# A three-layer block on one core: C's first values in other banks, dense groups ahead of scores and transposes, and norm roots as log and exp

## What is computed

```python
h = rmsnorm_2(x, pre_mix_w[l])
proj = h @ w_in[l]                       # q_a, k_a, v_a, q_b, k_b, v_b, gates
y_a = diff_attention(q_a, k_a, v_a, lam, subln_w[l], lambda_init)
y_b = neighbourhood_attention_2d(q_b, k_b, v_b, rpb[l])
merged = g_a * (y_a @ w_branch_a[l]) + g_b * (y_b @ w_branch_b[l])
x = x + rmsnorm_2(merged @ w_out[l], post_mix_w[l])
h = rmsnorm_2(x, pre_ffn_w[l])
f = (jax.nn.silu(h @ w_gate[l]) * (h @ w_up[l])) @ w_down[l]
x = x + rmsnorm_2(f, post_ffn_w[l])
```

## Time and profile before

| | us |
|---|---|
| median of 3 runs (lowest to highest) | 2002.32 (2001.63 to 2002.58) |
| profiled execution, its own time | 2001.68 |
| its span | 2000.0 |
| TensorE (PE) busy | 1973.4, 99% of the span |
| VectorE (DVE) busy | 1039.5, 52% |
| ScalarE (ACT) busy | 713.0, 36% |
| GpSimd (POOL) busy | 18.8, 1% |
| mean granted TensorE clock | 0.997 |

### The profile page before, as it was taken

How to read it: one execution, slowest core, us unless ns; L and a number is a source line. 1 busy time by engine, 2 the same in 40 slices (tenths; PEclk the granted TensorE clock), 3 DMA queues, 4 the chain that set the end, 5 groups by cost and what they waited for, 6 DMA issues and landing times.

```text
span 2000.0 us, 25477 instructions
## 1 busy us (share of the span) xinstructions
PE 1973.4 (99%) x9948; PEld 1608.8 (80%) x9948; DVE 1039.5 (52%) x1458; ACT 713.0 (36%) x1058; POOL 18.8 (1%) x57
## 2 busy tenths in 40 slices
PE   9999999999999999999999999999999999999998
PEld 7988888888887777778888887766778998888887
DVE  6354665425465455575434556665445585533544
ACT  5443432212243444442222233444433452223232
POOL 0100000000000000000000000000000000000000
PEclk9999999999999999999999999999999999999999
DMA  4321333343233222233333324112323323233322
GB/s 158 92 72 54 108 84 92 87 116 84 81 108 127 85 80 69 85 85 90 93 111 84 89 83 146 45 64 61 107 70 104 107 64 104 75 106 94 100 71 81
DMA packets 299983, 180.79 MB, mean 90 GB/s; under 512 B 19179, under 2 KB 295764, under 8 KB 299900
## 3 DMA queue, kind: packets, MB, share of 16 engines
q1 hardware_dynamic: 288959, 178.90, 30.7%
q10 hardware_dynamic: 10941, 0.75, 0.4%
HBM read 175.80 MB, written 2.75 MB: 89 GB/s over the span
## 4 chain that ended last, share of the span: by engine, by line
PE 91%; DVE 4%; ACT 3%; issue 1%; DMA 0%; DVEq 0%; ACTq 0%
PE psum L1731 28%; PE psum L1733 27%; PE psum L1732 27%; PE psum L1987 1%; DVE wl L1100 1%; PE psum L1940 1%; PE psum L1949 1%; PE psum L1912 1%; PE psum L1962 1%; PE psum L2024 1%; PE psum L1998 1%; ACT wh L620 1%; PE psum L1879 1%; PE psum L2006 1%; PE psum L2196 0%
## 5 line engine op out<-in xcount | busy, mean ns | idle before, releaser
L1100 DVE TENSOR_TENSOR wl<-stage,wh 128x2048 fp32r<-128x2048 f32 (+2 forms) x170 | 353.0, 2077 | 122.2 <-ACT wh L620 118.8
L620 ACT CAST wh<-stage 128x2048 fp32r<-128x2048 f32 (+2 forms) x164 | 283.4, 1728 | 230.2 <-PE psum L1733 221.0
L1731 PE MATMUL psum<-xl,wh 128*128 128x512 f32 (+1 forms) x768 | 304.9, 397 | 2.1 <-DVE work L1182 1.5
L1731 PE MATMUL psum<-x2l,wh 128*128 128x512 f32 x768 | 302.8, 394 | 1.0 <-DVE wl L1100 0.6
L1733 PE MATMUL psum<-x2h,wh 128*128 128x512 f32 x768 | 299.1, 389 | 0.0
L1732 PE MATMUL psum<-x2h,wl 128*128 128x512 f32 x768 | 299.0, 389 | 0.0
L1733 PE MATMUL psum<-xh,wh 128*128 128x512 f32 (+1 forms) x768 | 293.1, 382 | 0.0
L1732 PE MATMUL psum<-xh,wl 128*128 128x512 f32 (+1 forms) x768 | 292.5, 381 | 0.0
L1731 PE MATMUL psum<-hidl,wh 128*128 128x512 f32 x528 | 205.8, 390 | 2.6 <-DVE wl L1100 2.6
L1732 PE MATMUL psum<-hidh,wl 128*128 128x512 f32 x528 | 205.4, 389 | 0.0
L1733 PE MATMUL psum<-hidh,wh 128*128 128x512 f32 x528 | 205.4, 389 | 0.0
(11 more groups left out here) (344 smaller groups left out, 2621.9 us busy)
## 6 DMA issues: line engine op xcount, KB each, us to landing
stage<-in_ffn_w_gate_dram SPq DMA_DIRECT2D x44, 512.0 KB, 4.1
stage<-in_ffn_w_up_dram SPq DMA_DIRECT2D x44, 512.0 KB, 5.3
stage<-in_w_in_dram SPq DMA_DIRECT2D x40, 512.0 KB, 4.2
stage<-in_ffn_w_down_dram SPq DMA_DIRECT2D x32, 384.0 KB, 3.7
stage<-in_a_w_in_dram SPq DMA_DIRECT2D x22, 512.0 KB, 4.8
stage<-in_w_gate_dram SPq DMA_DIRECT2D x22, 512.0 KB, 4.1
stage<-in_w_up_dram SPq DMA_DIRECT2D x22, 512.0 KB, 5.3
stage<-in_ffn_w_down_dram SPq DMA_DIRECT2D x32, 320.0 KB, 3.6
```

The lines of the kernel that those rows point to most:

```text
L620: nc.scalar.copy(wh[:, par, 0:n], stage[:, par, 0:n]).then_inc(w_hi, 1)
L1100: vec.tensor_tensor(wl[:, par, 0:n], stage[:, par, 0:n], wh[:, par, 0:n].bitcast(F32), ALU.subtract).then_inc(w_lo, 1)
L1731: mm(out, a_hi, b_lo, start=start, stop=False)
```

## The change

- C_va0 is multiplied into banks 6 and 7, with no wait for an epilogue. The turn of `rs` in layer C runs behind it and into bank 4 (`TURN_BANK`). Its epilogue reads banks 6 and 7.
- In layer B the first dense group of step 0 goes ahead of that step's first scores.
- In the four sum steps of layer C two dense groups instead of one go ahead of the transposes. In the last of them, which has two sets of transposes, both sets stand together behind the second group.
- In the output projection the products of half block 0 with the last merged tile go behind nine matmuls of half block 1, which waits for one epilogue less. The sum for the first root goes behind four more products of half block 4.
- The four roots of the output projection (two token halves, two norms) are now made on ScalarE as exp(-0.5 * ln(x + eps)), two activations, and VectorE's four reciprocals go. The table set with both functions is loaded ahead of half block 0's epilogue.

```diff
+        TURN_BANK = {1: 6, 2: 4}
...
                 def mixer_root(h):
                     act.wait_ge(pm_sum, h + 1)
-                    nc.scalar.activation(rsm[:, HALF[h]], psum[:, 4 + h, HALF[h]], ACT.Sqrt, bias=eps[:, 0:1]
+                    nc.scalar.activation(rsm[:, HALF[h]], psum[:, 4 + h, HALF[h]], ACT.Ln, bias=eps[:, 0:1]
                                          ).then_inc(pm_root, 1)
+                    act.wait_ge(pm_root, h + 1)
+                    nc.scalar.activation(rsm[:, HALF[h]], rsm[:, HALF[h]], ACT.Exp, scale=-0.5).then_inc(pm_rs, 1)
...
                 split_out(2)
+                nc.scalar.preload_act_table_set(LN_EXP)
                 halves(0)
...
-                nc.scalar.copy(rst[:, :, :], psum[:, 6, 0:TT * 8].rearrange("p (t h) -> p t h", t=TT)).then_inc(rst_ready, 1)
+                nc.scalar.copy(rst[:, :, :], psum[:, TURN_BANK[n], 0:TT * 8].rearrange("p (t h) -> p t h", t=TT)).then_inc(rst_ready, 1)
...
-                ps = psum[:, 2 * par:2 * par + 2, :]
+                bank = 6 if name == "C_va0" else 2 * par
+                ps = psum[:, bank:bank + 2, :]
...
-                def mixer_rs(h):
-                    dve.wait_ge(pm_root, h + 1)
-                    vec.reciprocal(rsm[:, HALF[h]], rsm[:, HALF[h]]).then_inc(pm_rs, 1)
-                    dve.wait_ge(pm_rs, h + 1)
...
-            def multiply(name, b, par, first):
+            def multiply(name, b, par, first, bank=None):
...
-                if not isinstance(b, int) or b >= 2:
-                    pe.wait_ge(block_out, b - 1)
+                if bank is None:
+                    bank = 2 * par
+                    if not isinstance(b, int) or b >= 2:
+                        pe.wait_ge(block_out, b - 1)
...
                 turn_rs(1)
+                units_of(b_stream, 0, 0, 3)
                 for s in range(B_STEPS + 2):
...
-                    units_of(b_stream, s, 0, 3)
+                    if s:
+                        units_of(b_stream, s, 0, 3)
...
                 multiply("C_ka0", first + 1, 1, False)
+                multiply("C_va0", first + 2, 0, False, 6)
                 turn_rs(2)
-                multiply("C_va0", first + 2, 0, False)
                 pe.wait_ge(rst_ready, 3)
...
                     u = s - 1
+                    summing = 0 <= head < DA_HEADS and qt == 2
+                    if summing:
+                        units_of(c_stream, s, 1, 3)
...
-                        units_of(c_stream, s, a + 1, 3)
+                        if a or not summing:
+                            units_of(c_stream, s, a + 1, 3)
...
                     if h < 2:
-                        pe.wait_ge(block_out, cout + h - 1)
+                        pe.wait_ge(block_out, cout - 1)
...
                     if h == 0:
-                        for k in range(DT):
+                        for k in range(DT - 1):
                             for a in range(2):
-                                last = half_product(h, a, (k,))
+                                half_product(0, a, (k,))
+                        continue
+                    if h == 1:
+                        half_product(1, 0, range(3))
+                        half_product(0, 0, (DT - 1,))
+                        half_product(0, 1, (DT - 1,)).then_inc(cs_done, 1)
+                        half_product(1, 0, range(3, DT))
                     else:
                         half_product(h, 0)
-                        if h == 4:
-                            pe.wait_ge(cs_add, 8)
-                            mm(psum[:, 4, HALF[0]], ones[:, :], ss[:, HALF[0]], start=True, stop=True).then_inc(pm_sum, 1)
-                        last = half_product(h, 1)
-                    last.then_inc(cs_done if h < 4 else mm_done, 1)
+                    if h == 4:
+                        half_product(4, 1, range(4))
+                        pe.wait_ge(cs_add, 8)
+                        mm(psum[:, 4, HALF[0]], ones[:, :], ss[:, HALF[0]], start=True, stop=True).then_inc(pm_sum, 1)
+                    half_product(h, 1, range(4 if h == 4 else 0, DT)).then_inc(cs_done if h < 4 else mm_done, 1)
```

More of the change, by code:

```diff
@@ L927, in mixer_root @@
                     act.wait_ge(pm_sum, h + 1)
-                    nc.scalar.activation(rsm[:, HALF[h]], psum[:, 4 + h, HALF[h]], ACT.Sqrt, bias=eps[:, 0:1]
+                    nc.scalar.activation(rsm[:, HALF[h]], psum[:, 4 + h, HALF[h]], ACT.Ln, bias=eps[:, 0:1]
                                          ).then_inc(pm_root, 1)
+                    act.wait_ge(pm_root, h + 1)
+                    nc.scalar.activation(rsm[:, HALF[h]], rsm[:, HALF[h]], ACT.Exp, scale=-0.5).then_inc(pm_rs, 1)
                 def ffn_root(h):
                     act.wait_ge(xp_sum, h + 1)
-                    nc.scalar.activation(rs[:, HALF[h]], psum[:, 6 + h, HALF[h]], ACT.Sqrt, bias=eps[:, 0:1]
+                    nc.scalar.activation(rs[:, HALF[h]], psum[:, 6 + h, HALF[h]], ACT.Ln, bias=eps[:, 0:1]
                                          ).then_inc(xp_root, 1)
+                    act.wait_ge(xp_root, h + 1)
+                    nc.scalar.activation(rs[:, HALF[h]], rs[:, HALF[h]], ACT.Exp, scale=-0.5).then_inc(xp_rs, 1)
                 def tiles(h, t0, t1):
@@ L1289, in mixer_out @@
                 dve.wait_ge(fin_res, DT)
-                mixer_rs(0)
+                dve.wait_ge(pm_rs, 1)
                 tiles(0, 0, 2)
@@ L1300, in mixer_out @@
                 halves(7)
[L1301 removed]
+                dve.wait_ge(pm_rs, 2)
                 tiles(1, 0, 10)
[L1303 removed]
                 split(up20 + 2, 0, SLOT)
[L1305 removed]
                 vec.memset(ss[:, :], 0.0).then_inc(ss_zero, 1)
@@ L1774, in multiply @@
                     for t in range(TT):
-                        o = psum[:, 2 * par + t // 2, 256 * (t % 2):256 * (t % 2) + 256]
+                        o = psum[:, bank + t // 2, 256 * (t % 2):256 * (t % 2) + 256]
                         for k in range(kt):
@@ L2019, in attention_c @@
                             pe.wait_ge(t_out, i)
-                            if a == 0 and 0 <= head < DA_HEADS and qt == 2:
+                            if a == 0 and summing:
                                 pe.wait_ge(d_ln, head + 1)
@@ L2221, in turn_rs @@
                 for t in range(TT):
-                    last = nc.tensor.transpose(psum[:, 6, t * 8:(t + 1) * 8], rs[0:8, t * P:(t + 1) * P], ident[0:8, 0:8])
+                    last = nc.tensor.transpose(psum[:, TURN_BANK[n], t * 8:(t + 1) * 8], rs[0:8, t * P:(t + 1) * P], ident[0:8, 0:8])
                 last.then_inc(rst_t, 1)
```

6 lines of the change are left out of this document (removed).

## The result

The changed kernel takes 1991.78 us (median of 6 runs, 1989.94 to 1992.69). The kernel before takes 2002.02 (6 runs, 2001.63 to 2002.58). The ratio is 0.9948 with a 95% interval of 0.9938 to 0.9958. That is 10.2 us less; the forecast was 10.5 less and 1991.8. The profiled execution is the fastest of the six: 1989.94 with a span of 1988.2, which is 11.7 less than the profiled 2001.68 of before. The two differences are not the same; experiments 4 to 6 tell why. All medians leave out two executions in a much slower state (2072.12 in experiment 3, at a mean clock of 0.908, and 3193.17 in experiment 11, at 0.571).

The account below looks back on a forecast made before the run. TensorE, busy 99% of the span, was taken as the bound, so only its idle or low-clock time could be won. Terms -5.4 - 1.0 - 1.3 - 1.1 - 1.7 = -10.5 from 2002.32 gave 1991.8 us, range 1989.8 to 1995.8.

Parts of the forecast that it names:

- The start of C: Start of layer C: net gain 5.4 us, 6.6 won less 1.2 given back; bounds 3.85 and 6.6.
- the small edits: Layer B's first scores 1.0, sum steps 1.3, output projection's start 1.1 and roots 1.7 us less.
- Start of C, what is won: Layer C: C_va0 directly behind C_ka0 at full clock, turn and copy 0.8; first scores 6.6 us earlier.
- The rival in which C_va0 does not start early: Start of layer C: C_va0's operands hold it until the norm, only small edits pay: 1997.2 us; chance 0.04.
- Start of C, what comes back: Layer C, first transposes: VectorE's list is no shorter, so TensorE newly waits about 1.2 us, once.
- VectorE sets the pace: Rival, start of layer C: first steps chase VectorE, gain 3.85 in place of 5.4: 1993.4 us; chance 0.16.
- the clock rival: Start of layer C: clock drops all the same; 24 low matmuls 1994.0 us, all 96 cost 8.9, 2000.7; chance 0.06.
- First scores of layer B: Layer B, step 0: a dense group covers the 0.97 wait for B_q0's epilogue; 1.0 us less.
- Sum steps: Layer C's four sum steps: waits of 1.9 and 0.2 go, a new 0.8 comes; 1.3 us less.
- Start of the output projection: Output projection: nine matmuls cover the wait for the last merged tile, table load costs nothing; 1.1 us less.
- Roots: Output projection: without the last reciprocal the stall before the first up epilogue goes; 1.7 us less.
- the rival on the slower side: Attention steps of layer C: clock flickers at short holes; four low-clock steps give 2015 us; chance 0.02.

Follow-up runs that it names:

- experiment 4: The changed kernel again, unchanged, for a second profile: 1990.59 us, ratio 0.9944.
- experiment 5: The changed kernel with VectorE's eight residual updates moved one at a time into later steps of layer C: 1990.83 us, ratio 0.9943.
- experiment 6: The changed kernel with the load of C_qa1's weights issued ahead of the 32 small bias loads: 1989.72 us, ratio 0.9942.
- experiment 3: The kernel before with 15 unread matmuls in the stall between C_ka0 and the turn: 1999.71 us, ratio 0.9988.
- experiment 11: The changed kernel with residual updates later, C_qa1's weights first, last sum step as before, 8 unread matmuls in the last wait, one table load: 1988.69 us, ratio 0.9934.
- experiment 10: The changed kernel with a second table load (1.28 us) ahead of half block 0's epilogue: 1993.53 us in one run.
- experiment 2: The changed kernel with the start of layer C put back as before: 1995.78 us, ratio 0.9969.
- experiment 7: The changed kernel with a dense group back between the two sets of transposes in the last sum step: 1990.96 us, ratio 0.9945.
- experiment 8: The changed kernel with square root and reciprocal back in the output projection, without the added table load: 1994.21 us, ratio 0.9961.
- experiment 1: The kernel before with only the start of layer C changed: 1997.41 us, ratio 0.9975.

## Why the prediction was right, and where it was not

**The number and the sign** hold: 1991.8 forecast, 1991.78 measured, ratio 0.9948. But errors offset each other in it, and that the median is met to 0.02 is luck: the same kernel has a median of 1990.59 in experiment 4. The start of C gives less in six of the seven profiles than the forecast's 5.4 (4.2 to 5.3; 5.9 in the first), the small edits give more than its 5.1 (5.6), and the tail, which the sum leaves out, gives 0.6 in some executions and takes up to 1.4 in others (10.2 to 12.2 from the first sum to the end in the changed kernel and its variants, 10.8 before).

**Start of C, what is won: right.** 6.6 forecast, 6.6 measured. C_va0 starts directly behind C_ka0, the clock stays at 1.00, turn and copy take 0.69 from the turn's start to the scores (0.8 forecast), and the copy wait of 0.28 is the gap that was announced as 0.4. The rival in which C_va0 does not start early is out.

**Start of C, what comes back: the mechanism right, the size not.** The forecast had one fixed number, 1.2, for VectorE's list. It is 0.7 in the fastest execution (a wait of 0.52 where 1.2 was expected); in experiment 4 the step-2 scores stand 25.98 behind C_ka0's last matmul of 512 columns (1235.35), and 30.37 in the kernel before: 4.4 net, so 2.2 came back of 6.6. It was also not "paid once": with a late cast TensorE waits at the scores of step 1 too (0.96, then 0.99 at the transposes). The step that failed is the sentence "No DMA is added or moved. SyncE's loads are released by VectorE's weight splits, which come earlier with the rest; the transfers have room." The load at issue is not released by the split alone: it stands in a queue behind 32 issues of 21.4 to 23.1 us in all that no earlier TensorE work shortens, and with TensorE's stall gone the slack that had hidden this was gone too. The rival "VectorE sets the pace" had the right engine, but for all executions and at 3.85; it was nearly reached in the later ones, and its cause was a transfer. One price of the clock rival is mis-summed: 96 matmuls at 0.09 more are 8.6, not 8.9.

**First scores of layer B:** 1.0 forecast, 0.84 measured.

**Sum steps: the mechanism right, the term too small.** 1.3 forecast, 2.0 measured (0.81 + 0.84 + 0.82 - 0.44). I took the idle time alone, 1.9 over three steps. Each stall was worth some 0.2 more than its idle time (0.82 for 0.63), which I had counted at the output projection as the filling of the pipe and not here. The new wait for ScalarE's copy shows as 0.66 of idle; from when the second set was due, as the forecast counts, it is 0.9 (1376.15 against 1375.01 + 0.25) where 0.8 was forecast. It made the last step 0.44 worse where 0.6 was forecast.

**Start of the output projection:** 1.1 forecast, 1.07 measured; the table load costs nothing there, with 0.4 of cover left (experiment 10). **Roots:** 1.7 forecast, 1.69 measured; undone in the new order they cost 2.7.

**The clock and the rival on the slower side.** The clock did not fall at the start of C, in any profile that has this part of the change, and it did not go back and forth in the attention steps: two waits of 1.0 in a row left it at 1.00. The rule of the Trainium skill that the forecast weighed there (TensorE: Matmul & The Clock Gate, "A second HAM failure mode: psum-queue depth-cycling") does not show in any run here. What the forecast did not price is the other place where the clock was already low, the tail; it excepted it in its last part with the words "anywhere but at the end". That place is worth up to 2 us, and it differs by execution in the changed kernel, while of the runs of before in the experiments' sets all but two have a mean clock of 0.997, and they lie closer together. The six runs of experiment 2, with C's old start, lie within 0.56. The profiled 1989.94 had the short tail and the early cast both, which is why it is 11.7 ahead and the median only 10.2.

Left open: why the tail's clock differs between executions of the same kernel with the same wait of 2.17 ahead of it. With the wait filled, both profiles taken had turns of 3.69 and none of the ten executions in the medians a mean clock of 0.998; what decides it without the filling stays open.

## What to carry to other kernels

A stall of the busiest engine costs its idle time, the filling of the pipe behind it, and, where the granted clock falls in it, the work that then runs at the lower level: here 4.3 of idle time cost 6.6. When you remove a stall, look for what it had been hiding, and follow it through to the queue that issues the loads: the next limit was VectorE's list, whose start was set by a transfer queued behind 32 small ones that nobody needed yet. Where a stall can't be removed, matmuls that nobody reads can be cheaper than idleness, and one profile of a kernel whose runs spread should be read beside a second one: here the first was the fastest of the six, and hid what the others lost.

## What was not expected of the hardware

- The tail has the same 2.17 us wait in every profile without the filling, and different outcomes behind it: the 32 turns take 3.69 (the changed kernel, experiments 2 and 5), 5.07 to 5.36 (before, experiments 4, 7 and 8; the sums at 1.33 in 7), or 6.12 to 6.26 with the eight sums at 1.80 to 1.88 instead of 1.06 (experiments 1, 3, 6 and 10). From the first sum to the end of the span this is 10.2, 10.6 to 11.1, and 12.1 to 12.2. With 8 unread matmuls in the wait they took 3.69 in both profiles taken.
- 32 loads of 16 partitions each take SyncE 21.4 to 23.1 us to issue, 0.67 to 0.72 each, and differ by up to 1.7 us between executions; a load behind them is issued as much later.
- 15 unread matmuls in a wait made the kernel 2.4 us faster (0.9988, 0.9978 to 0.9998), for the clock stayed at 1.00 behind them.
